# GELU gate by exponential and division, weight split on GpSimd, and row work one step later in a two-block transformer kernel

## The chip, the cores and the metric

The kernel runs on one core of a Trainium2 chip. The metric is the device time of one execution in microseconds (us). The core's engines are TensorE (PE in the profile, with its weight loads as PEld), VectorE (DVE), ScalarE (ACT), GpSimd (POOL) and SyncE (SP), which only issues DMAs here. Each engine works through its own instructions in program order and waits on semaphores for the others.

## What is computed

Two transformer blocks over 1024 rows of 1024 numbers in float32: first an mLSTM and pooling layer and a windowed attention layer, then a block with gated linear attention, differential attention and a feed-forward part with a convolution. The change touches the code of that feed-forward part and the schedule of the output projections. In short:

```python
# the end of each mixer: a product with w_out, added to x, then the norm of the next part
h = h + jnp.concatenate([o_gla, o_diff], axis=-1) @ w_out[i]
h = h + conv_ffn(rms_norm(h, norm_ffn[i]), w_up[i], conv_w[i], conv_b[i], w_down[i])

def conv_ffn(h, w_up, conv_w, conv_b, w_down):       # w_up is 1024 x 5632, w_down 2816 x 1024
    T = h.shape[1]
    u = h @ w_up
    up = jnp.pad(u, ((0, 0), (CONV_W - 1, 0), (0, 0)))
    c = conv_b + sum(up[:, j:j + T] * conv_w[j] for j in range(CONV_W))      # CONV_W = 3
    gate, val = jnp.split(c, 2, axis=-1)
    return (jax.nn.gelu(gate) * val) @ w_down
```

## The kernel before

**Split weights.** Products are made from pairs: each 128x4096 weight slot holds a high part (ScalarE's rounded copy, `split_hi`, L403) and a low part (VectorE's difference, `split_lo`, L412), and TensorE sums three passes of high and low. The same is done for the other operand. There are three weight slots, `K.W[:, 0..2]`, loaded by SyncE; a slot is loaded again when TensorE has finished with its old item.

**Output projections (`rows_part`).** `out0`, `out1`, `out2` and `down` are built by one function. Rows come in tiles of 128; `out1` and `out2` have three groups of tiles, [0,1,2], [3,4,5] and [6,7], with `per` = 4 weight items for each group, so 12 steps s = 0..11. `out0` has `per` = 8 and `down` `per` = 11. After a group's last step its tiles go through this sequence, all 128x1024:

- VectorE adds the old x (L2622 in `out2`; L2629 and L2633 in `out1`), ScalarE makes the norm factor (`act_x`, L559), VectorE scales the tile ("scale", `vec_scale`, L588);
- TensorE turns it by eight 128x128 transposes into the one PSUM tile `TR` ("turn r", `pe_turn`, L633). Turn r waits until the tile before it was read from `TR` (semaphore `ht_done`);
- VectorE multiplies `TR` by the norm gain ("value r", `vec_value`, L610; this raises `ht_done`), ScalarE rounds it ("high r", L618), VectorE makes the difference ("low r", L624).

Which tile is handled at which step is said by `due(s, lag, behind)`. Turns come at lag 1, at the end of a step: tiles 3, 4, 5 are turned at the ends of steps 9, 10 and 11. Value and high use lag 2, low uses lag 3, each one step more where `behind` applies. Within one step VectorE's order is: low parts that are due; adds; the split of this step's weights; at s = 11 also the split of the first item of the next part (`following[0]` in `out1`; `tail[2](v, 0)`, the first up-projection weights, in `out2`); scale; value. The next part's first item can only be loaded once step 9's weights are free.

**Up projection (`up_part`).** 22 column tiles j. For each, `w_up` brings 128 gate and 128 value columns (two DMAs), double buffered in two of the three weight slots: `load_up` for tile j waits until TensorE finished tile j-2. ScalarE makes the high part (`up_w_hi`, L3515) and VectorE the low one (`up_w_lo`, L3520). TensorE makes unit (j, 0), the gate half, and (j, 1), the value half, each 48 matmuls in four PSUM buffers of two banks. For tiles 0 and 1 it makes the first 512 rows of all four units (interleaved with the last two turns of `out2`), then the second 512 rows. Per half, ScalarE takes the centre tap from PSUM (L3627) and VectorE adds the other two (L3652, L3654). The gate then goes: square on ScalarE (L3632), one product on VectorE (L3667), four functions on ScalarE (L3634 to L3637: Relu, Exp, Ln, Exp, which give a sigmoid), the gate product on VectorE (L3669), and at the end the product with the value half (L3676). `down` starts when the last tile's units are made; its step 1 needs weights and operands that VectorE splits after it has finished tile 21 (L3676).

GpSimd issues the loads and stores of x rows (`B.queue`, L526 and L530) and waits at the end of each `rows_part` until all stores have landed; it does no arithmetic in the parts from `out1` on but for two masks.

Of the kernel before, what the change touches and what calls it, by code (L numbers as in the profile page):

```python
# [29 lines left out]
ALU = mybir.AluOpType  # L30
ACT = mybir.ActivationFunctionType
# [2399 lines left out]
def rows_part(K, st, name, key, groups, turned, source, n_store, gg_rows=None, stream=None, ready=None, raw=None, raw_at=0,  # L2431
# [13 lines left out]
    def due(s, lag, behind=0):  # L2445

        for g, rs in enumerate(groups):
            stride = 2 if per >= 8 and g + 1 < len(groups) else 1
            inside = per * (g + 1) + 4 + stride * (len(rs) - 1) < len(steps)
            wait = lag + behind if inside else lag  # L2450
            n, late = divmod(s - per * (g + 1) - wait, stride)
            if late == 0 and 0 <= n < len(rs):
                yield rs[n]
# [160 lines left out]
    def vector(v):  # L2614
# [20 lines left out]
        for s in range(len(steps) + 6):  # L2635
# [6 lines left out]
            if s == len(steps) and following:  # L2642
                K.split_lo(v, following[1])
            if s == len(steps) + 3 and tail is not None:
                tail[2](v, 1)
            for r in ended(s)[:1] if per >= 8 else ended(s):
# [886 lines left out]
def up_part(K, st, rows):  # L3533
# [19 lines left out]
    s_c, s_sq, s_arg, s_e, s_at = (K.sem("up_centre"), K.sem("up_square"), K.sem("up_gelu_arg"),  # L3553
                                   K.sem("up_gelu_sigmoid"), K.sem("up_act_ready"))

# [11 lines left out]
    def sync(sp):  # L3567
        for j in range(2, NJ):
            K.wait_unit(sp, ("up", j - 2, 1))
            load_up(K, sp, j, K.up_in[j % 2])  # L3570
        for j in (NJ - 2, NJ - 1):
            K.wait_unit(sp, ("up", j, 1))
            K.load_item(sp)
        sp.wait_ge(s_cg, 1)

    def tensor(pe):
# [35 lines left out]
    def scalar(a):  # L3612
        ch = Chain(a, K.a_chain, K.an)
        rows.done(a)
        for j in range(NJ):
            if 2 <= j and j + 1 < NJ:
                up_w_hi(K, a, j + 1)
# [3 lines left out]
            for half, c in ((0, cg), (1, cv)):  # L3621
# [7 lines left out]
                if half == 0:  # L3629
                    K.wait_read(a, key)  # L3630
                    at = K.AT[:, j, :]
                    a.activation(at, cg[:, j % 2, :], ACT.Square, scale=math.sqrt(CUBE)).then_inc(s_sq, 1)  # L3632
                    a.wait_ge(s_arg, j + 1)
                    ch.link(a.activation(at, at, ACT.Relu, scale=SLOPE, bias=K.cut[:, :]))  # L3634
                    ch.link(a.activation(at, at, ACT.Exp, scale=-1.0, bias=K.cut[:, :]))
                    ch.link(a.activation(at, at, ACT.Ln, bias=K.one[:, :]))
                    a.activation(at, at, ACT.Exp, scale=-1.0).then_inc(s_e, 1)  # L3637
                    if j == 0:
                        up_w_hi(K, a, 2)
        K.an = ch.n  # L3640

    def vector(v):
        ch = Chain(v, K.v_chain, K.vn)
        rows.done(v)

        def conv(j, half, c):
# [11 lines left out]
        for j in range(NJ):  # L3658
            at, g = K.AT[:, j, :], cg[:, j % 2, :]
            if 2 <= j and j + 1 < NJ:  # L3660
                up_w_lo(K, v, j + 1)
            if j == NJ - 1:
# [3 lines left out]
            v.wait_ge(s_sq, j + 1)  # L3666
            v.scalar_tensor_tensor(out=at, in0=at, scalar=1.0, in1=g, op0=ALU.add, op1=ALU.mult).then_inc(s_arg, 1)  # L3667
            v.wait_ge(s_e, j + 1)
            ch.link(v.tensor_tensor(at, at, g, ALU.mult))  # L3669
            if j == 0:  # L3670
                up_w_lo(K, v, 2)
            if j == NJ - 1:
# [17 lines left out]

    return Part(sync, None, tensor, scalar, vector, None, (), None, done, taken, left)

# [186 lines left out]
def phase_gla_in(K):  # L3879
# [17 lines left out]
    with ExitStack() as st:  # L3897
# [13 lines left out]
        @block.gpsimd  # L3911
        def _(g):
            out1.gpsimd(g)
            diff.gpsimd(g)
            out2.gpsimd(g)
            down.gpsimd(g)
            ple.gpsimd(g)
# [65 lines left out]
```

## Time and profile before

| | |
|---|---|
| median of 3 runs | 3419.11 us (3415.29 to 3421.77) |
| profiled execution | 3419.11 us, its span 3417.3 us |
| PE busy | 3295.9 us (96%) |
| DVE busy | 1765.1 us (52%) |
| ACT busy | 1508.5 us (44%) |
| POOL busy | 100.3 us (3%) |
| mean granted TensorE clock | 0.988 |

The span runs from the first to the last instruction; 1.8 us of the profiled execution lie around it. Busy times are sums over the whole program and say little of a single part: `out1` lies at about 1863 to 1966 us, `out2` ends at 2520, the up projection ends at 3015, and `down` follows.

### The profile page before, as it was taken

The numbers are of one execution on the slowest core, as the hardware profiler recorded it, in microseconds if no ns is written. First come the engines' busy times: TensorE is split into PE (matmuls) and PEld (weight loads), VectorE is DVE, ScalarE is ACT, GpSimd is POOL, SyncE is SP. The second block draws the span as 40 slices with busy tenths as digits, with TensorE's granted clock in tenths as the row PEclk, the third lists the DMA queues.
The fourth block names the chain that finished last, engine by engine and source line by source line (L and its number), as shares of the span: only waits on it lengthen the run. The fifth ranks groups of instructions, "written<-read, shape, count | busy, mean of one in ns | idle before, by whom it ended". The sixth has DMA issues, their size and how long they took to land. (4 is left out here: it accounts for less than half of the span.)

```text
span 3417.3 us, 42752 instructions
## 1 busy us (share of the span) xinstructions
PE 3295.9 (96%) x17536; PEld 2667.1 (78%) x17536; DVE 1765.1 (52%) x2730; ACT 1508.5 (44%) x2409; POOL 100.3 (3%) x224
## 2 busy tenths in 40 slices
PE   6999999999999999999999999998999999999997
PEld 4988888888777777888787777776778888878775
DVE  6644444445344367541886644348555444544544
ACT  4343433435323345215786534227435444443454
POOL 0000000000000000001000000000000000000000
PEclk9999999999999999999999999999999999999998
DMA  5102011121333456222301711010332111134453
GB/s 202 58 13 81 28 53 56 41 68 38 141 105 134 174 207 249 67 50 68 94 2 34 195 56 50 26 54 1 124 112 61 49 43 44 50 130 160 177 186 129
DMA packets 188533, 308.38 MB, mean 90 GB/s; under 512 B 28369, under 2 KB 122643, under 8 KB 188211
## 3 DMA queue, kind: packets, MB, share of 16 engines
q1 hardware_dynamic: 166275, 226.27, 20.6%
q0 software_dynamic: 19424, 74.14, 6.0%
q10 hardware_dynamic: 2640, 5.24, 0.4%
q8 instruction: 139, 2.28, 0.3%
q14 instruction: 55, 0.45, 0.0%
HBM read 269.87 MB, written 35.75 MB: 89 GB/s over the span
## 5 line engine op out<-in xcount | busy, mean ns | idle before, releaser
L412 DVE TENSOR_TENSOR W_rounded<-W,W_rounded 128x2048 fp32r<-128x2048 f32 (+1 forms) x172 | 348.8, 2029 | 443.4 <-ACT W_rounded L403 440.3
L403 ACT ACTIVATE W_rounded<-W 128x2048 fp32r<-128x2048 f32 (+1 forms) x172 | 292.4, 1701 | 398.6 <-DMA W<-in_w_down 96.9
L3583 PE MATMUL G<-HT_rounded,W_rounded 128*128 128x512 f32 x1584 | 452.7, 393 | 0.0
L3583 PEld LDWEIGHTS G<-HT_rounded,W_rounded 128*128 128x128 f32 x1584 | 298.3, 188 | 68.4
L2547 PE MATMUL G<-W_rounded,r_y_rounded 128*128 128x512 f32 x960 | 229.4, 399 | 6.4 <-DVE r_y_rounded L2653 5.1
L2547 PE MATMUL G<-W_rounded,x_hi 128*128 128x512 f32 x704 | 221.1, 395 | 3.6 <-DVE act_turned_rounded L2653 3.4
L2547 PEld LDWEIGHTS G<-W_rounded,r_y_rounded 128*128 128x128 f32 x960 | 181.1, 190 | 51.7 <-DVE W_rounded L412 6.2
L1147 PE MATMUL G<-W_rounded,HT_rounded 128*128 128x512 f32 x640 | 213.7, 415 | 0.0
L2200 PE MATMUL G<-HT_rounded,W_rounded 128*128 128x512 f32 (+1 forms) x768 | 209.2, 357 | 2.9 <-DVE W_rounded L412 2.9
L3583 PE MATMUL G<-HT_lo_ffn,W_rounded 128*128 128x512 f32 x528 | 208.5, 395 | 0.0
L1191 PE MATMUL G<-HT_rounded,W_rounded 128*128 128x512 f32 (+1 forms) x768 | 205.7, 354 | 1.0 <-PEq L651 1.0
L2870 PE MATMUL G<-W_rounded,HT_rounded 128*128 128x512 f32 x640 | 203.1, 399 | 0.0
L2547 PEld LDWEIGHTS G<-W_rounded,x_hi 128*128 128x128 f32 x704 | 132.4, 189 | 35.3 <-DVE W_rounded L412 4.4
L2200 PEld LDWEIGHTS G<-HT_rounded,W_rounded 128*128 128x128 f32 x768 | 137.5, 189 | 28.2 <-DVE W_rounded L412 3.9
L1191 PEld LDWEIGHTS G<-HT_rounded,W_rounded 128*128 128x128 f32 x768 | 136.0, 188 | 22.6 <-issue 1.2
L2870 PEld LDWEIGHTS G<-W_rounded,HT_rounded 128*128 128x128 f32 x640 | 118.4, 188 | 28.2 <-issue 2.0
L2547 PE MATMUL G<-W_rounded,act_turned_rounded 128*128 128x512 f32 x352 | 139.9, 397 | 0.0
L1147 PEld LDWEIGHTS G<-W_rounded,HT_rounded 128*128 128x128 f32 x640 | 120.2, 188 | 25.2
L2200 PE MATMUL G<-HT_lo,W_rounded 128*128 128x512 f32 (+1 forms) x384 | 137.1, 357 | 0.0
L1191 PE MATMUL G<-HT_lo,W_rounded 128*128 128x512 f32 (+1 forms) x384 | 136.4, 355 | 0.0
L1646 PE MATMUL G<-W_rounded,HT_rounded 128*128 128x512 f32 x416 | 131.6, 397 | 0.2 <-DVE W_rounded L412 0.2
L2870 PE MATMUL G<-W_rounded,o_turned_lo 128*128 128x512 f32 x320 | 126.1, 394 | 0.0
(461 smaller groups left out, 6456.3 us busy)
## 6 DMA issues: line engine op xcount, KB each, us to landing
W<-in_w_down SPq DMA_DIRECT2D x33, 1024.0 KB, 4.8
W<-in_ab_w_out SPq DMA_DIRECT2D x32, 1024.0 KB, 5.5
W<-in_w_up SPq DMA_DIRECT2D x44, 512.0 KB, 5.1
W<-in_ab_w_in SPq DMA_DIRECT2D x20, 1024.0 KB, 8.1
W<-in_w_mod SPq DMA_DIRECT2D x8, 2048.0 KB, 8.2
x_rows<-r_xt POOLq DMA_DIRECT2D x32, 512.0 KB, 5.4
W<-in_c_w_out SPq DMA_DIRECT2D x24, 512.0 KB, 7.2
r_xt<-x_rows POOLq DMA_DIRECT2D x24, 512.0 KB, 4.8
```

Of the source, the lines that this page charges most:

```text
L403: ins = a.activation(self.half(key, True)[:, at], self.half(key, False, False)[:, at], ACT.Copy)
L412: ins = v.tensor_tensor(self.half(key, False)[:, at], self.half(key, False, False)[:, at], self.half(key, True)[:, at].bitcast(F32), ALU.s ...
L1147: ins = pe.matmul(G[:, K.par(key), :], x[y][:, 4 * kh + k, r * P:(r + 1) * P], wv[z][:, k, :], start=(kh == 0 and k == 0 and (y, z) == SPL ...
L1191: ins = pe.matmul(G[:, K.par(key), 0:n], wv[y][:, k, cc], x[z][:, k, c0:c0 + n], start=(k == 0 and (y, z) == SPLIT_PASSES[0]), stop=(k == ...
L1646: ins = pe.matmul(bank(key), x[y][:, 4 * kh + k, r * P:(r + 1) * P], w[z][:, k, :], start=(kh == 0 and k == 0 and (y, z) == SPLIT_PASSES[0 ...
L2200: ins = pe.matmul(bank(key, n), w[y][:, k, cc], x[z][:, k, c0:c0 + n], start=(k == 0 and (y, z) == SPLIT_PASSES[0]), stop=(k == KT - 1 and ...
L2547: ins = pe.matmul(slot(r)[:, n * 512:(n + 1) * 512], x[y], w[z][:, k, n * 512:(n + 1) * 512], start=(kk == 0 and k == 0 and (y, z) == SPLI ...
L2870: ins = pe.matmul(bank(key), x[y][:, 4 * kh + k, r * P:(r + 1) * P], w[z][:, k, :], start=first, stop=last)
L3583: ins = pe.matmul(bank(("up", j, half))[:, rc * 512:rc * 512 + 512], w[a][:, k, c], x[b][:, 2 * rc:2 * rc + 2, :], start=(k == 0 and a == ...
```

## The change

Three things are changed. In `up_part` the sigmoid is made as 1 / (1 + exp(-SLOPE z)): one exponential on ScalarE, then an addition of 1 and a reciprocal on VectorE; the cubic argument is made by VectorE in two instructions. The low parts of the up-projection weights for j = 1 to 21 are made by GpSimd (a new `gpsimd` function that stands behind `out2`'s in GpSimd's queue), and `up_w_hi(2)` moves from the inside of iteration 0 to the head of iteration 1. In `rows_part`, `due` gives the extra step to every group but the last. For `out0` (`per` 8) and `down` (`per` 11) the old and the new rule give the same steps; for `out1` and `out2` the values, highs and lows of tiles 3, 4, 5 move from steps 10, 11, 12 (values, highs) and 11, 12, 13 (lows) to one step later each.

```diff
--- before.py
+++ after.py
@@ -2445,9 +2445,8 @@
     def due(s, lag, behind=0):
 
         for g, rs in enumerate(groups):
+            wait = lag + behind if g + 1 < len(groups) else lag
             stride = 2 if per >= 8 and g + 1 < len(groups) else 1
-            inside = per * (g + 1) + 4 + stride * (len(rs) - 1) < len(steps)
-            wait = lag + behind if inside else lag
             n, late = divmod(s - per * (g + 1) - wait, stride)
             if late == 0 and 0 <= n < len(rs):
                 yield rs[n]
@@ -2641,8 +2640,6 @@
                         B.vec_lo(v, r)
             if s == len(steps) and following:
                 K.split_lo(v, following[1])
-            if s == len(steps) + 3 and tail is not None:
-                tail[2](v, 1)
             for r in ended(s)[:1] if per >= 8 else ended(s):
                 add(r)
             if s < len(steps):
@@ -3551,7 +3548,7 @@
     first = K.pl.units[("up", 0, 0)]
     s_cg = K.sem("up_last_gate")
     s_c, s_sq, s_arg, s_e, s_at = (K.sem("up_centre"), K.sem("up_square"), K.sem("up_gelu_arg"),
-                                   K.sem("up_gelu_sigmoid"), K.sem("up_act_ready"))
+                                   K.sem("up_gelu_exp"), K.sem("up_act_ready"))
 
     def bank(key):
         return G[:, (K.pl.units[key] - first) % 4, :]
@@ -3572,6 +3569,10 @@
             K.wait_unit(sp, ("up", j, 1))
             K.load_item(sp)
         sp.wait_ge(s_cg, 1)
+
+    def gpsimd(g):
+        for j in range(1, NJ):
+            up_w_lo(K, g, j)
 
     def tensor(pe):
         def piece(j, half, rc):
@@ -3610,10 +3611,9 @@
                 piece(j, half, 1).then_inc(K.gemm_done, 1)
 
     def scalar(a):
-        ch = Chain(a, K.a_chain, K.an)
         rows.done(a)
         for j in range(NJ):
-            if 2 <= j and j + 1 < NJ:
+            if 1 <= j and j + 1 < NJ:
                 up_w_hi(K, a, j + 1)
             if j == NJ - 1:
                 K.split_hi(a, ("down", 0, 0))
@@ -3628,21 +3628,13 @@
                              bias=K.col("conv_b_2", tile)).then_inc(s_c, 1)
                 if half == 0:
                     K.wait_read(a, key)
-                    at = K.AT[:, j, :]
-                    a.activation(at, cg[:, j % 2, :], ACT.Square, scale=math.sqrt(CUBE)).then_inc(s_sq, 1)
+                    a.activation(K.AT[:, j, :], cg[:, j % 2, :], ACT.Square).then_inc(s_sq, 1)
                     a.wait_ge(s_arg, j + 1)
-                    ch.link(a.activation(at, at, ACT.Relu, scale=SLOPE, bias=K.cut[:, :]))
-                    ch.link(a.activation(at, at, ACT.Exp, scale=-1.0, bias=K.cut[:, :]))
-                    ch.link(a.activation(at, at, ACT.Ln, bias=K.one[:, :]))
-                    a.activation(at, at, ACT.Exp, scale=-1.0).then_inc(s_e, 1)
-                    if j == 0:
-                        up_w_hi(K, a, 2)
-        K.an = ch.n
+                    a.activation(K.AT[:, j, :], K.AT[:, j, :], ACT.Exp, scale=-SLOPE).then_inc(s_e, 1)
 
     def vector(v):
         ch = Chain(v, K.v_chain, K.vn)
         rows.done(v)
-
         def conv(j, half, c):
 
             key = ("up", j, half)
@@ -3657,18 +3649,17 @@
 
         for j in range(NJ):
             at, g = K.AT[:, j, :], cg[:, j % 2, :]
-            if 2 <= j and j + 1 < NJ:
-                up_w_lo(K, v, j + 1)
             if j == NJ - 1:
                 K.split_lo(v, ("down", 0, 0))
                 K.early[1](v)
             conv(j, 0, cg)
             v.wait_ge(s_sq, j + 1)
-            v.scalar_tensor_tensor(out=at, in0=at, scalar=1.0, in1=g, op0=ALU.add, op1=ALU.mult).then_inc(s_arg, 1)
+            ch.link(v.tensor_scalar(at, at, CUBE, 1.0, ALU.mult, ALU.add))
+            v.tensor_tensor(at, at, g, ALU.mult).then_inc(s_arg, 1)
             v.wait_ge(s_e, j + 1)
+            ch.link(v.tensor_scalar(at, at, 1.0, None, ALU.add))
+            ch.link(v.reciprocal(at, at))
             ch.link(v.tensor_tensor(at, at, g, ALU.mult))
-            if j == 0:
-                up_w_lo(K, v, 2)
             if j == NJ - 1:
                 v.tensor_copy(K.zcol[:, 1:2], K.eps[:, :]).then_inc(s_cg, 1)
             conv(j, 1, cv)
@@ -3688,7 +3679,7 @@
 
         K.wait_unit(eng, ("up", NJ - 1, 1))
 
-    return Part(sync, None, tensor, scalar, vector, None, (), None, done, taken, left)
+    return Part(sync, gpsimd, tensor, scalar, vector, None, (), None, done, taken, left)
 
 
 def phase_up(K):
@@ -3913,6 +3904,7 @@
             out1.gpsimd(g)
             diff.gpsimd(g)
             out2.gpsimd(g)
+            up.gpsimd(g)
             down.gpsimd(g)
             ple.gpsimd(g)
 
```

## Rows read from the trace of the kernel before

**Rows 1.** Windows of all engines: busy us of PE, PEld, DVE, ACT, POOL, clock, DMA.
```profile
2600.00:3000.00 400.00, 400.00 (x1734) 325.21 (x1733) 204.54 (x148) 182.29 (x148) 0.00 (x0) 1.00 0.17 48
```

**Rows 2.** Timeline of PE, `out1`'s end: start us, us, engine, line, operation, [idle before <-releaser].
```profile
1958.12 1.03 PE L633 MATMUL TR<-ident,r_xs 128*128 128x128 f32 x8
...
1978.30 1.09 PE L633 MATMUL TR<-ident,r_xs 128*128 128x128 f32 x8 [1.26 <-DVE r_xs L588]
```

**Rows 3.** Timeline of ACT, the high part of `out1`'s `following[0]`.
```profile
1957.22 1.92 ACT L403 ACTIVATE W_rounded<-W 128x2048 fp32r<-128x2048 f32 x1 [0.31 <-DMA W<-in_w_in]
```

**Rows 4.** Timeline of DVE, `out1`'s step 11.
```profile
1956.95 4.52 DVE L412 TENSOR_TENSOR W_rounded<-W,W_rounded 128x2048 fp32r<-128x2048 f32 x2 [0.58 <-ACT W_rounded L403]
...
1962.05 1.21 DVE L610 TENSOR_TENSOR r_h_turned<-TR,cols 128x1024 f32<-128x1024 f32 x1
```

**Rows 5.** Timeline of DVE, `out2`'s step 11: first up split, scale 5, value 4.
```profile
2515.20 2.29 DVE L3520 TENSOR_TENSOR W_rounded<-W,W_rounded 128x2048 fp32r<-128x2048 f32 x1 [3.92 <-ACT W_rounded L3515]
2517.41 0.75 DVE L588 TENSOR_SCALAR r_xs<-r_xt,r_ss 128x1024 f32<-128x1024 f32 x1
2518.07 1.22 DVE L610 TENSOR_TENSOR row_room<-TR,cols 128x1024 f32<-128x1024 f32 x1
```

**Rows 6.** Timeline of PE, `out2`'s end: the turns of tiles 4 to 7.
```profile
2510.23 1.03 PE L633 MATMUL TR<-ident,r_xs 128*128 128x128 f32 x8
...
2519.44 1.06 PE L633 MATMUL TR<-ident,r_xs 128*128 128x128 f32 x8 [2.23 <-DVE row_room L610]
...
2529.18 1.97 PE L633 MATMUL TR<-ident,r_xs 128*128 128x128 f32 x8 [3.16 <-DVE r_xs L588]
...
2538.26 1.03 PE L633 MATMUL TR<-ident,r_xs 128*128 128x128 f32 x8
```

**Rows 7.** Windows of PE alone behind two of its waits: PE busy, clock, DMA, GB/s.
```profile
1945.00:1952.00 7.00, 7.00 (x27) 0.81 0.86 239
...
2529.00:2535.00 6.00, 5.82 (x18) 0.52 0.27 107
```

**Rows 8.** DMA issues of the page: KB each, median us from issue to landing.
```profile
x_rows<-r_xt POOLq DMA_DIRECT2D x32, 512.0 KB, 5.4
```

**Rows 9.** Groups of POOL by line and shape: busy us, mean ns, idle before.
```profile
L1060 POOL MEMSET k_rows<- 68x1280 f32 x1 | 1.2, 1164 | 70.8 <-POOLq L651 70.8
```

**Rows 10.** Timeline of ACT, high part of the up weights of tile 2.
```profile
2567.13 1.92 ACT L3515 ACTIVATE W_rounded<-W 128x2048 fp32r<-128x2048 f32 x1 [0.19 <-DMA W<-in_w_up]
```

**Rows 11.** Timeline of PE where unit (1, 1) ends and (2, 0) begins.
```profile
2570.72 2.01 PE L3583 MATMUL G<-HT_rounded,W_rounded 128*128 128x512 f32 x8
```

**Rows 12.** Timeline of DVE, the split before tile 21 to `down`'s step 1.
```profile
3000.38 2.29 DVE L412 TENSOR_TENSOR W_rounded<-W,W_rounded 128x2048 fp32r<-128x2048 f32 x1 [1.63 <-ACT W_rounded L403]
...
3005.90 1.28 DVE L3652 SCALAR_TENSOR_TENSOR W<-G,cols,W 128x1023 f32<-128x1023 f32 x1 [2.36 <-ACT W L3627]
...
3009.63 1.23 DVE L3667 SCALAR_TENSOR_TENSOR act_turned<-act_turned,W 128x1024 f32<-128x1024 f32 x1 [1.13 <-ACT act_turned L3632]
3015.53 1.23 DVE L3669 TENSOR_TENSOR act_turned<-act_turned,W 128x1024 f32<-128x1024 f32 x1 [4.67 <-ACT act_turned L3637]
...
3019.62 1.23 DVE L3676 TENSOR_TENSOR act_turned<-act_turned,W 128x1024 f32<-128x1024 f32 x1
3022.55 2.29 DVE L412 TENSOR_TENSOR W_rounded<-W,W_rounded 128x2048 fp32r<-128x2048 f32 x1 [1.71 <-ACT W_rounded L403]
```

**Rows 13.** Groups by line and shape: a reciprocal of two columns, the gate product, ScalarE's last Exp.
```profile
L1994 DVE RECIPROCAL sums<-sums 128x2 f32<-128x2 f32 x64 | 10.2, 160 | 2.2 <-ACT HT L1954 2.2
...
L3669 DVE TENSOR_TENSOR act_turned<-act_turned,W 128x1024 f32<-128x1024 f32 x22 | 26.9, 1225 | 102.9 <-ACT act_turned L3637 102.9
...
L3637 ACT ACTIVATE act_turned<-act_turned 128x1024 f32<-128x1024 f32 x22 | 23.3, 1060 | 0.7
```

**Rows 14.** Instructions of line 922: min/median/max ns, first and last start.
```profile
L922 DVE RECIPROCAL silu_c<-silu_c x1: 253/253/253, 13.9 to 13.9; 128x16 f32<-128x16 f32 x1
```

**Rows 15.** Timeline of PE, `down`'s step 1.
```profile
3025.86 0.82 PE L2547 MATMUL G<-W_rounded,x_hi 128*128 128x512 f32 x2 [1.92 <-DVE act_turned_rounded L2653]
```

## Prediction

> **What bounds the kernel now.** I read the windows of all engines first: how full is each engine where the change works, and at which clock? Over 400 us of the up projection TensorE is busy for all 400 at full clock, with 1734 matmuls, so 0.231 us each and 22.1 us for the 96 of a column tile, while DVE has 205 us of work and ACT 182 [rows 1]. There the path to the end is TensorE's own queue. Taking work off ScalarE or VectorE brings nothing in that stretch; time can only be lost or won where TensorE waits. So I read TensorE's timeline around every place that the change touches (the ends of `out1` and `out2`, the first tiles of the up projection, the step into `down`), and then, for each wait, the timelines of DVE and ACT to see what was late.
>
> **The extra step for tiles 3 to 5, in `out1`.** Turn 4 stands at the end of step 10 and needs value 3, since `TR` is one tile. Before, value 3 was made in VectorE's step 10 and turn 4 ran at 1958.12 without a wait [rows 2]. After, value 3 stands in step 11, behind that step's split, the split of `following[0]`, and scale 5. This slot is held by a load: the high part of `following[0]` starts at 1957.22 when its DMA has landed, ends at 1959.14 [rows 3], the low part takes half of the 4.52 of two splits [rows 4], to 1961.4, then scale 5 at 0.75 [rows 5]. The slot is thus the one where value 4 stood, 1962.05 to 1963.26 [rows 4]. Turn 4 can start at about 1963.4, 5.3 us late, and behind TensorE nothing else can go: step 11 and turn 5 queue behind it. Given back: the wait of 1.26 at turn 6 [rows 2], as ScalarE and VectorE catch up while TensorE stands. The matmuls behind a wait run partly at the lower clock level: behind a wait of 3.16 us [rows 6] the windows show a mean clock of 0.52 over 6 us, 2.9 us lost; behind one of 2.95 us, 0.81 over 7 us, 1.3 us lost [rows 7]. For the longer waits of this change I take 2.9, with 1.3 as the lower end. `out1`: 5.3 - 1.3 + 2.9 = **+6.9**.
>
> **The same in `out2`.** Value 3 moves behind `tail[2](v, 0)`, which waited 3.92 us for ScalarE's high part (and that for its DMA) and began at 2515.20; scale 5 follows, and the slot at 2518.07 is value 4's now [rows 5]. It released turn 5 at 2519.44; after, the same slot releases turn 4 at 2519.44, which used to run at 2510.23 [rows 6]. The wait is 9.2 us and swallows the old one of 2.23. Step 11 and one turn are left to do that before were done: 24 matmuls x 0.231 and eight transposes in about 1 us [rows 6], 6.5 us. By then scale 6 and value 5 are made (two adds, scale, value, some 5 us of VectorE), so the wait of 3.16 at turn 6 [rows 6] goes. Its lower clock goes too (2.9) and comes back behind the longer wait (2.9). `out2`: 6.5 - 3.2 = **+3.3**; lower end 1.7 with 1.3 for the clock.
>
> The removed `tail[2](v, 1)` frees 2.3 us of VectorE behind turn 6, where TensorE then waits for nothing: 0. GpSimd makes that low part instead, behind its wait until the last store has landed, 5.4 us after its issue [rows 8]. The last add is at about 2529, so it can start near 2535 and has until turn 7 is over, 2538.26 [rows 6] + 3.3 + 1.0 = 2542.6: 7 us for one instruction. That costs nothing below that price.
>
> **The low parts on GpSimd.** No row shows a two-input operation on POOL. Its memset writes 1280 columns in 1.164 us [rows 9], so 2048 columns are 1.86 us for one stream; a subtraction moves three streams, 5.6 us if each takes its turn. I take 4.5, near the upper end, since the memset reads nothing. The page GPSIMD Engine Reference of the Trainium skill, section 3.1, gives 4.5 us for a two-input operation of this size on GpSimd against 2.3 on VectorE; the trace shows only the VectorE side. In the steady state this hides: the weights of tile 2 landed 5.9 us after the unit that freed them (2567.13 less 2572.34 - 11.1) [rows 10, 11]; from tile 3 on TensorE needs them 22.1 us after that unit, and 22.1 - 5.9 - 1.9 = 14.3 are left for GpSimd; without that cover each tile would pay the excess. The tight place is tile 2, whose weights can be loaded only when unit (0, 1) is done, 11 us before they are needed. The high part starts at 2567.13 when the DMA has landed, and ends at 2569.05 [rows 10]. Of the eight matmuls from 2570.72 the last is the first of unit (2, 0), so it is at 2572.34 [rows 11]. With two handovers of 0.1 us, 3.1 us are left. Stall: 4.5 - 3.1, about **+1.5** (ends 0 and 2.6). `up_w_hi(2)` at the head of iteration 1 stands behind the centre tap of unit (0, 1), which is over before the DMA lands: 0.
>
> **The gate.** Between the start of L3667 and that of L3669 lie 5.90 us before [rows 12]. After, the same stretch holds an addition and scaling 0.75 and a product 1.23, one Exp 1.06, an addition 0.75 [rows 5, 12, 13], and a reciprocal of 1024 columns. Sixteen columns took 0.253 us, two 0.160 [rows 13, 14]: 6.6 ns a column, 6.9 us. The ends are far: 1.2 if it ran like a product, 16 if the whole 0.253 were columns. I take the slope. Sum 10.7, with handovers 10.9: +5.0 for each tile. VectorE then works about 19.7 us a tile (15.0 before, from 3005.90 to 3020.85 [rows 12], plus 5.0 less a wait of 0.3), below 22.1, so the up projection stays TensorE's, with 2.4 us to spare.
>
> **The step into `down`.** Tile 20 ends 5.0 late; the gaps of 1.63 and 2.36 around the split [rows 12] take 4.0 and a 0.3 of wait inside the tile, so tile 21 starts 0.7 late and ends 5.7 late. Then `down`'s step-1 split no longer waits 1.71 for ScalarE [rows 12]. TensorE's wait of 1.92 [rows 15] grows by 5.7 - 1.7 = **+4.0**. For the clock I add half of 2.9 - 1.3: **+0.8**. Lower end 0 (a cheap reciprocal), upper 6.5.
>
> **Sum.** 6.9 + 3.3 + 1.5 + 4.0 + 0.8 = 16.5 us. The profiled execution took 3419.11 with a span of 3417.3, 1.8 around it, and is itself the median: **3435.6 us**, 0.48% slower. About 0.2% (6.8 us) is what a measurement of this kernel can tell from no change.
>
> **Rivals.**
> - *The turns do not wait.* If value 3 were made before TensorE asks, only 1.5 + 4.8 remain: 3425.4. It decides at 1958.1 and 2510.2, so loads would have to land 5 and 9 us earlier. The releasers speak against it. This is the one that ends on the other side, not slower by 0.2%. Chance 0.07.
> - *The longer waits cost no clock.* With nothing lost behind either turn wait: 16.5 - 2.9 - 2.9 - 0.8 = +9.9, 3429.0. Chance 0.1.
> - *GpSimd and VectorE hold each other up.* Each low part on GpSimd meets a two-input product of VectorE. A product held for up to 4.5 us, less the 2.4 spare in a tile, ends tile 21 some 2 us later, and a held start at tile 2 adds up to 1.2: 3438.8. Nothing before has both engines at work, so the trace is silent. This is what SBUF — State Buffer in the Trainium skill, section "Who interferes with whom", would have: a VectorE instruction with two SBUF inputs and a GpSimd one that reads SBUF exclude each other. Chance 0.2.
> - *GpSimd is far slower than its bound,* 9 us or more (held at each step): tile 2 waits 6, with 2.9 of clock, and VectorE is pushed by up to 4.5 at the end: +12 on the sum, 3448. It would set the pace only above 14.3. Chance 0.08.
> - *VectorE becomes the bound.* Above a reciprocal of 9.3 us its tile exceeds 22.1; at 10.3 some 20 tiles lose 1 us each: 3456. The slope speaks against it. Chance 0.05.
> - *My sum:* 0.5.
>
> **Range.** 3424 to 3447 takes in the first three rivals with the lower ends (5.3 + 1.7 + 0 + 0 = 7.0, 3426) and the upper ones. Slower by over 0.2%: my sum, the second to the fifth rival, less their low edges: 0.85. Within: 0.12, from the first rival and the low ends together. Faster: 0.03, since no wait before leaves 7 us to win at these places.
>
> **What would show it.** In the new profile: turn 4 of `out1` (L633) waits about 5 us, and of `out2` about 9, for the value in L610; turn 6 in both waits for nothing; clock windows below 1 behind both; a POOL TENSOR_TENSOR of some 4.5 us at L3520, 21 times; TensorE waits about 1.5 us for it at tile 2 and never after; a RECIPROCAL of about 6.9 us, 22 times; TensorE waits about 6 us at `down`'s step 1. I am wrong if value 3 is reached earlier, if the reciprocal's slope does not hold at 1024 columns, or if DVE instructions stretch beside POOL's.

## The result

The changed kernel took 3439.14 us (median of 4 runs, 3433.74 to 3442.89), the kernel before 3420.34 us beside it (4 runs). The ratio is 1.0054, with a 95% interval of 1.0041 to 1.0066: slower by 18.8 us by the medians and by 14 to 22.6 by the interval. The prediction had 3435.6 us in a range of 3424 to 3447. The profiled execution took 3436.55 us, its span 3434.8.

### The profile page after: what moved, and what is told of

Its sections match the earlier page's. It is cut to its first block and busy times, and to the rows that moved or that the text cites. A ratio compares the mean times of both kernels' runs of the same rounds, so it can differ in the third digit from the quotient of the medians.

```text
span 3434.8 us, 42754 instructions
## 1 busy us (share of the span) xinstructions
PE 3296.7 (96%) x17536; PEld 2668.0 (78%) x17536; DVE 1944.5 (57%) x2775; ACT 1430.8 (42%) x2343; POOL 198.2 (6%) x245
## 5 line engine op out<-in xcount | busy, mean ns | idle before, releaser
L1191 PEld LDWEIGHTS G<-HT_rounded,W_rounded 128*128 128x128 f32 x768 | 136.0, 188 | 22.6 <-issue 1.2
L3661 DVE RECIPROCAL act_turned<-act_turned 128x1024 f32<-128x1024 f32 x22 | 144.2, 6553 | 0.8
```

The lines of the kernel that those rows point to most:

```text
L1191: ins = pe.matmul(G[:, K.par(key), 0:n], wv[y][:, k, cc], x[z][:, k, c0:c0 + n], start=(k == 0 and (y, z) == SPLIT_PASSES[0]), stop=(k == ...
L3661: ch.link(v.reciprocal(at, at))
```

## The profile after

Where the 17.5 us between the two spans arose is read from TensorE's timeline, at places that both kernels have: the first matmul of `out1` and of `down`, and the turns of tiles 3 and 7. The places of before that [rows 2, 6] do not show are from the same timeline. Each stretch is the difference of two starts.

| stretch on TensorE | before | after | difference |
|---|---|---|---|
| start to `out1` | 1863.84 | 1865.38 | +1.5 |
| `out1` to its turn 7 | 120.97 | 123.83 | +2.9 |
| to `out2`'s turn 3 | 518.95 | 517.12 | -1.8 |
| to `out2`'s turn 7 | 34.50 | 37.24 | +2.7 |
| to `down`'s start | 477.27 | 478.75 | +1.5 |
| `down` to the end of the span | 401.8 | 412.5 | +10.7 |

The first and the third row hold hardly any instruction that the change touches: 1.5 and -1.8 us there are the scatter of one execution against another. The second row mixes the change with such scatter. Up to the turn of tile 3, ahead of any moved instruction, `out1` took 87.9 us before and 85.1 after; from there to the turn of tile 7 it took 33.1 and 38.8. So the change itself costs 5.7 us in `out1`. The prediction had 6.9, 3.3, 1.5 and 4.8 for the four others.

The page of the changed kernel, busy time and share by engine (its first and third line):

```profile
span 3434.8 us, 42754 instructions
...
PE 3296.7 (96%) x17536; PEld 2668.0 (78%) x17536; DVE 1944.5 (57%) x2775; ACT 1430.8 (42%) x2343; POOL 198.2 (6%) x245
```

TensorE's work is the same as before (3295.9). DVE has 179 us more, ACT 78 less, POOL 98 more. TensorE is idle for 138.1 us of the span, 121.4 before. These 16.7 us are nearly all of the 17.5; its busy time, which holds what a lower clock costs anywhere in the program, grew by 0.8.

The timeline of PE, both turns of tile 4; columns as in [rows 2]:

```profile
1961.82 1.94 PE L633 MATMUL TR<-ident,r_xs 128*128 128x128 f32 x8 [4.20 <-DVE r_h_turned L610]
```

```profile
2521.91 1.94 PE L633 MATMUL TR<-ident,r_xs 128*128 128x128 f32 x8 [8.94 <-DVE row_room L610]
```

Where [rows 2, 6] have turn 4 without a wait, it waits now for value 3, in both parts. Turn 6, which waited 1.26 and 3.16 us, waits for nothing. These two turns take 1.94 us each, where [rows 2] has 1.03: the clock is low, as it was for the turn behind 3.16 us in [rows 6]. The windows of PE alone behind them, and behind the first matmul of `down`'s step 1 (columns as in [rows 7]):

```profile
1961.00:1969.00 8.00, 7.18 (x25) 0.61 0.13 51
...
2521.00:2529.00 8.00, 7.09 (x25) 0.62 0.00 0
...
3039.00:3047.00 8.00, 7.03 (x19) 0.57 0.10 41
3047.00:3053.00 6.00, 6.00 (x28) 1.00 0.10 14
```

Behind each of the three waits the engine is busy 7 of 8 us at a mean clock near 0.6, so at 1.2 GHz for most of the stretch, and is back at 2.4 GHz in the next 6 us. That is some 3 us each, as [rows 7] had behind a wait of 3.16.

Why value 3 comes late stands in DVE's timeline at the end of `out1` and of `out2`:

```profile
1957.58 2.29 DVE L412 TENSOR_TENSOR W_rounded<-W,W_rounded 128x2048 fp32r<-128x2048 f32 x1 [2.43 <-ACT W_rounded L403]
1959.79 0.75 DVE L588 TENSOR_SCALAR r_xs<-r_xt,r_ss 128x1024 f32<-128x1024 f32 x1
1960.45 1.22 DVE L610 TENSOR_TENSOR r_h_turned<-TR,cols 128x1024 f32<-128x1024 f32 x1
...
2517.68 2.29 DVE L3517 TENSOR_TENSOR W_rounded<-W,W_rounded 128x2048 fp32r<-128x2048 f32 x1 [5.29 <-ACT W_rounded L3512]
2519.88 0.75 DVE L588 TENSOR_SCALAR r_xs<-r_xt,r_ss 128x1024 f32<-128x1024 f32 x1
2520.55 1.22 DVE L610 TENSOR_TENSOR row_room<-TR,cols 128x1024 f32<-128x1024 f32 x1
```

The slot is the predicted one: behind a split that waits for the next part's weights, and behind scale 5. In `out1` that load landed 1.6 us earlier (ScalarE's high part starts at 1955.63, not 1957.22 as in [rows 3]), and TensorE was ready for the turn 0.5 us earlier, so the wait is 4.20 and not 5.3.

Now the step into `down`. TensorE's list of waits from 2560 to 3060 us is short (engine, tile, line, releaser: total us, times, longest):

```profile
PE G L2546 <- DVE act_turned_rounded L2650: 9.2, 1, 9.2
PE G L3584 <- POOL W_rounded L3517: 1.2, 1, 1.2
```

The second is tile 2, predicted at 1.5. The first was 1.92 [rows 15] and predicted at about 6; here is the step that went wrong. The groups of the up projection by line and shape (busy us, mean ns, idle before), first two of VectorE, then one of GpSimd:

```profile
L3661 DVE RECIPROCAL act_turned<-act_turned 128x1024 f32<-128x1024 f32 x22 | 144.2, 6553 | 0.8
L3662 DVE TENSOR_TENSOR act_turned<-act_turned,W 128x1024 f32<-128x1024 f32 x22 | 76.3, 3469 | 0.8
...
L3517 POOL TENSOR_TENSOR W_rounded<-W,W_rounded 128x2048 fp32r<-128x2048 f32 x21 | 97.5, 4644 | 359.8 <-ACT W_rounded L3512 357.3 <-DMA x_rows<-r_xt 2.4
```

Two prices that the old trace did not show came out near their estimates: the reciprocal 6.55 us (6.9), GpSimd's subtraction 4.64 (4.5). But the gate product, 1.225 us in [rows 13], has a mean of 3.47. One tile of it in the timelines of DVE and POOL:

```profile
2980.63 6.55 DVE L3661 RECIPROCAL act_turned<-act_turned 128x1024 f32<-128x1024 f32 x1
2987.22 4.15 DVE L3662 TENSOR_TENSOR act_turned<-act_turned,W 128x1024 f32<-128x1024 f32 x1
2991.40 1.28 DVE L3644 SCALAR_TENSOR_TENSOR W<-G,cols,W 128x1023 f32<-128x1023 f32 x1
```

```profile
2985.66 4.62 POOL L3517 TENSOR_TENSOR W_rounded<-W,W_rounded 128x2048 fp32r<-128x2048 f32 x1 [17.46 <-ACT W_rounded L3512]
```

GpSimd starts during the reciprocal and ends at 2990.28. The product starts at 2987.22 and ends at 2991.37, 1.1 us after GpSimd's end, which is about its own usual length: it makes no headway until GpSimd's instruction is over. The same is seen in the 20 tiles whose product overlaps a low part of GpSimd: each product ends 1.07 to 1.10 us after GpSimd's instruction, however long it has been under way (1.33 to 4.69 us). The page SBUF — State Buffer of the Trainium skill, section "Who interferes with whom", says that a VectorE instruction with two SBUF inputs and a GpSimd one that reads SBUF exclude each other; the trace agrees, with these numbers.

What the holds leave behind, in DVE's timeline of tiles 20 (first line) and 21:

```profile
3009.30 1.23 DVE L3662 TENSOR_TENSOR act_turned<-act_turned,W 128x1024 f32<-128x1024 f32 x1
...
3017.41 1.28 DVE L3644 SCALAR_TENSOR_TENSOR W<-G,cols,W 128x1023 f32<-128x1023 f32 x1
...
3035.53 1.23 DVE L3667 TENSOR_TENSOR act_turned<-act_turned,W 128x1024 f32<-128x1024 f32 x1
3036.67 2.28 DVE L412 TENSOR_TENSOR W_rounded<-W,W_rounded 128x2048 fp32r<-128x2048 f32 x1
```

`down` starts at 3022.32 on TensorE. Against that, tile 21's first tap starts at -4.9 (before -9.6, from 3005.90 and 3015.53 in [rows 12] and the table) and its last product at +13.2 (before +4.1). So VectorE comes to tile 21 4.7 us late, the gate adds 4.4, together 9.1. The two gaps of 1.63 and 2.36 us in [rows 12] are gone, and so is the one of 1.71 before the last split. 9.1 less 1.8 for that last one is 7.3, and 1.92 + 7.3 is the wait of 9.2.

The 4.7 us are not the last hold alone. The table has how much later than in the kernel before VectorE starts a tile's first tap, each kernel measured from its own first matmul of `down` (us; `pool_later`, an experiment below, keeps GpSimd's low parts off the product from tile 10 on):

| tile | 3 | 4 | 5 | 10 | 11 | 12 | 20 | 21 |
|---|---|---|---|---|---|---|---|---|
| changed kernel | 6.8 | 5.7 | 4.8 | 4.7 | 4.7 | 4.7 | 4.7 | 4.7 |
| `pool_later` | 6.8 | 5.8 | 4.9 | 4.8 | 1.8 | 0.0 | 0.0 | 0.1 |

VectorE comes late out of the first tiles. Where nothing holds it, it makes up 3 us a tile. In the changed kernel the hold takes just these 3 us from each tile: a product that starts 1.0 us after GpSimd takes 4.69 us, one that starts 2.0 us after it 3.68. So VectorE stays behind to the end.

## The experiments

Each kernel is compared with the kernel before on the same chip. Line numbers are those of each kernel and differ by a few.

### Each part alone

`rows_only` is the kernel before with the new `due`; `gate_and_pool` is the changed kernel with the old one. `gate_only` puts only the new gate into the kernel before. `pool_only` is `gate_and_pool` with the old gate.

```diff
 # in short
 rows_only                     (gate_and_pool: the reverse, in the changed kernel)
-            inside = per * (g + 1) + 4 + stride * (len(rs) - 1) < len(steps)
-            wait = lag + behind if inside else lag
+            wait = lag + behind if g + 1 < len(groups) else lag
 gate_only
-        Square, scalar_tensor_tensor, Relu, Exp, Ln, Exp
+        Square, tensor_scalar, tensor_tensor, Exp, tensor_scalar, reciprocal
 pool_only                     (against the kernel before)
+    def gpsimd(g):
+        for j in range(1, NJ):
+            up_w_lo(K, g, j)
```

> The kernel before with nothing but the new rule in due (values, highs and lows of tiles 3 to 5 one step later in out1 and out2). My theory: this is a part of its own, worth what the markers of the changed kernel show for it: TensorE's offset to before grows by about 3 us over out1 (turn 4 waits about 4, turn 6 no longer waits) and by about 2.7 us over out2 (turn 4 waits 9, the waits of 2.2 and 3.2 go), so +6 us, 3426. Rival A (the later values cost nothing by themselves and only matter beside GpSimd's part): within 1 us of before. Rival B (the clock behind the waits makes it dearer): +9 to +10 as I had summed.

> The changed kernel with the old rule in due. My theory: the rest of the loss, +1.2 at tile 2 and +7 to +10 at down's step 1 with its clock, so +10 to +12 us, 3431; the wait at down's step 1 stays at about 9 us. Rival (the parts lean on each other): the wait at down is near 6 and the sum of this run and rows_only is more than 3 us away from the whole change's 17 to 19.

> The kernel before with the gate by exponential and reciprocal, but low parts of the up weights on VectorE as before, old order, old due. VectorE's tile is then 19.5 us plus the low part's 2.3, 21.8, just under TensorE's 22.1. My theory: no instruction of VectorE is stretched (products at 1.22 us), but its low parts come late at tiles 2 and 3 (waits of about 3 us each, with some lower clock) and the wait at down's step 1 is 5 to 7 us: +10 to +13 us. Rival (the reciprocal alone is harmless as long as GpSimd does not touch SBUF): +4 or less, from down's step 1 alone.

> The changed kernel with the old gate (four functions on ScalarE, no reciprocal) and the old due: only the low parts are on GpSimd. My theory: VectorE has 9 us to spare per tile, so a held product costs nothing; TensorE waits about 1.2 us at tile 2, the wait at down's step 1 is near its old 1.9: +1 to +2 us, within noise of before. Rival (GpSimd's part alone makes the loss by holding VectorE): the wait at down's step 1 grows to 5 or more and the time by +5 or more.

| kernel | median us (runs) | before us | ratio | interval |
|---|---|---|---|---|
| `rows_only` | 3429.87 (5) | 3416.83 | 1.0034 | 1.0021 to 1.0047 |
| `gate_and_pool` | 3429.17 (8) | 3416.83 | 1.0037 | 1.0024 to 1.0049 |
| `gate_only` | 3428.55 (11) | 3416.83 | 1.0033 | 1.0021 to 1.0045 |
| `pool_only` | 3421.14 (12) | 3416.83 | 1.0009 | 0.9998 to 1.0020 |

TensorE's waits of `rows_only` at the end of `out1`, at the end of `out2`, and at `down`:

```profile
PE TR L633 <- DVE r_h_turned L610: 5.2, 1, 5.2
...
PE TR L633 <- DVE row_room L610: 9.1, 1, 9.1
...
PE G L2546 <- DVE act_turned_rounded L2652: 2.1, 1, 2.1
```

Those of `gate_and_pool` at `out2` and from 2560 us on, and last that of `gate_only` at `down`:

```profile
PE TR L633 <- DVE r_xs L588: 3.1, 1, 3.1
PE TR L633 <- DVE row_room L610: 1.8, 1, 1.8
...
PE G L2547 <- DVE act_turned_rounded L2651: 9.4, 1, 9.4
PE G L3585 <- POOL W_rounded L3518: 1.4, 1, 1.4
...
PE G L2547 <- DVE act_turned_rounded L2653: 4.5, 1, 4.5
```

The waits part cleanly. The new `due` alone makes the two waits of turn 4 and leaves `down` at 2.1; the gate with GpSimd leaves `out2` as it was and makes 9.4 at `down`. `gate_only` has 4.5 at `down`, its gate product takes 1.225 us on the mean, and its waits at tiles 2 and 3 come to 3.8 us, for VectorE's low parts this time. `pool_only` has 1.9 at `down` and 2.0 at tile 2, and no time that its interval tells from no change; it also holds the moved `up_w_hi(2)` and the removed `tail[2](v, 1)`. Its held instruction is the final product of a tile (mean 1.71 us), and VectorE has the slack for it. So neither half of the second part makes the 9.4 by itself: the gate alone gives 4.5, GpSimd alone nothing, both together 9.4.

Against the expectations: `gate_and_pool` (10 to 12 expected) and `gate_only` (10 to 13) came about as expected, +12.3 and +11.7 us, though the wait of `gate_only` at `down` is 4.5 and not 5 to 7. `rows_only` did not: 6 us were expected, read off two rows of the first table, and it lost 13.0, at least 7 by its interval. `pool_only` has 4.3 by the medians where 1 to 2 were expected, with an interval of -0.7 to 6.8.

In `rows_only`, `out1` to its turn 7 took 126.57 us and `out2` from turn 3 to turn 7 37.44: +5.6 and +2.9 against before, where the changed kernel had +2.9 and +2.7. From turn 3 to turn 7 of `out1` the two kernels agree, +6.2 and +5.7. The difference lies ahead of turn 3 and can be read: in the 75 us from 1860 on, ahead of any moved instruction, the profiled execution of before and that of `rows_only` had a mean granted clock of 0.95, that of the changed kernel 0.98, which is 2.2 us of head start for the latter.

The two halves come to 13.0 and 12.3 us by their medians and the whole to 18.8, whose interval ends at 22.6. The intervals of the halves, 7 to 16 and 8 to 17 us, allow that. Of the rival that the parts lean on each other, one sign came (the sum is more than 3 us off) and the other did not (the wait at `down` stays 9.4). Whether a few us are shared between the halves is not settled by these runs.

### Is it the hold?

`pool_later` is `gate_and_pool` with GpSimd's low part held back, from tile 12 on, until VectorE has made the final product of tile j - 2; what it meets then are taps, whose one tensor input is in PSUM and the other in SBUF, and not the gate product. `no_reciprocal` is `gate_and_pool` with the reciprocal replaced by a minimum with 1.0; it leaves out the division of the gate.

```diff
 pool_later
         for j in range(1, NJ):
+            if j >= 12:
+                g.wait_ge(s_at, j - 1)
             up_w_lo(K, g, j)
 no_reciprocal
-            ch.link(v.reciprocal(at, at))
+            ch.link(v.tensor_scalar(at, at, 1.0, None, ALU.min))
```

> As gate_and_pool, but from tile 12 on GpSimd starts a low part only when VectorE has finished the tile two before, so that its instruction no longer falls on the gate product behind the reciprocal. My theory (VectorE's product is held until GpSimd's instruction has ended): the product at that place drops from 4.2 us to 1.22 from there on, VectorE's last tile ends about 3 us earlier, the wait at down's step 1 falls from 9.4 to about 6 as I had predicted, and with it the time by 3 to 4 us against gate_and_pool; GpSimd still finishes before TensorE asks. Rival (VectorE's lateness at the end comes from the reciprocal alone, the long product only fills a gap): the product gets short but the wait at down stays above 8.5.

> As gate_and_pool, with the reciprocal replaced by a minimum with 1.0 of the same shape, which leaves the division out (the gate factor is then 1). My theory: VectorE's tile falls to about 14 us, GpSimd's low part meets no two-input product any more, the wait at down's step 1 goes back to about 2, and what is left against before is the 1.4 of tile 2: +1 to +2 us. Rival (GpSimd's low part holds VectorE wherever it falls): stretched VectorE instructions remain and the wait at down stays at 4 or more.

`pool_later` took 3423.82 us (12 runs) against 3416.71, ratio 1.0020 (1.0009 to 1.0030). `no_reciprocal` took 3417.07 (10 runs), 0.9998 (0.9987 to 1.0008). Of `pool_later`, the timeline of DVE at the tile shown above, then that of POOL, then the wait at `down`:

```profile
2976.17 6.55 DVE L3664 RECIPROCAL act_turned<-act_turned 128x1024 f32<-128x1024 f32 x1
2982.76 1.23 DVE L3665 TENSOR_TENSOR act_turned<-act_turned,W 128x1024 f32<-128x1024 f32 x1
...
2990.80 1.28 DVE L3647 SCALAR_TENSOR_TENSOR W<-G,cols,W 128x1023 f32<-128x1023 f32 x1 [2.91 <-ACT W L3630]
```

```profile
2987.96 4.62 POOL L3518 TENSOR_TENSOR W_rounded<-W,W_rounded 128x2048 fp32r<-128x2048 f32 x1 [17.52 <-DVE act_turned L3670]
```

```profile
PE G L2547 <- DVE act_turned_rounded L2651: 4.5, 1, 4.5
```

Nothing changed but the time at which GpSimd starts, from tile 12's low part on. The product is back at 1.23 us, VectorE has 2.91 us of slack in a tile again, and the wait at `down` falls from 9.4 to 4.5, which is what `gate_only` had. By the medians that is 12.3 to 7.1 us of loss; the two intervals overlap, so the time alone would not settle it, but the product and the wait do; in the two profiles `down` to the end of the span takes 409.0 and 405.0 us. The instruction on GpSimd takes 4.62 us whether it meets the product or not: where GpSimd has started first, only VectorE gives way. The expectation had about 6 left at `down`; 4.5 were.

`no_reciprocal` keeps GpSimd early. Its low parts take 4.61 us, a few final products are held (mean 1506 ns), and `down` waits 2.1 us. The expectation had no held product left; but with the 6.55 us out of VectorE's tile, a hold finds slack to fall into and costs nothing that is measured. So the loss at `down` needs the reciprocal, which alone takes the wait from 1.9 to 4.5; the hold takes it from there to 9.4.

### The order of VectorE's queue in step 11

If turn 4 of `out2` waits only because value 3 stands behind the split for the next part, then that split moved behind scale and value should give the time back, with the new `due` still in place. `rows_tail_last` does so to `rows_only`, `tail_last` to the kernel before.

```diff
-                if tail is not None:
-                    tail[2](v, 0)
 ...                                   # scale and value of this step
+            if s == len(steps) - 1 and tail is not None:
+                tail[2](v, 0)         # and the same for ScalarE's tail[1](a, 0)
```

> As rows_only (new rule in due), but in out2's step 11 both halves of the first up split stand behind scale, value and high of that step, on ScalarE and on VectorE. My theory (value 3 is late only because it stands behind a split that waits for a load): the wait at out2's turn 4 falls from 9.1 to about 2, out1 keeps its 5.2, and out2's part of the loss goes: +7 or so in all instead of +11. Rival (the extra step itself, not what stands in it, is the price): turn 4 still waits 8 or more.

> The kernel before with the same order of step 11 in out2 (the first up split behind scale, value and high), old due. If the waits at out2's end come from work standing behind the load of the first up weights, turn 5 no longer waits 2.2, turn 6 waits less than 3.2, the lower clock behind them may go, and the kernel is 2 to 6 us faster than before, near what can be measured. Rival (the first up weights are then late themselves): TensorE waits for L3520 at unit (0, 0) instead and the time is the same.

`rows_tail_last` took 3421.77 us (10 runs) against 3416.71, ratio 1.0009 (0.9997 to 1.0020), where `rows_only` had 1.0034. Its waits at the end of `out2`, and its values 3 and 4 in DVE's timeline:

```profile
PE TR L633 <- DVE row_room L610: 3.6, 3, 1.7
PE G L3582 <- DVE W_rounded L3519: 1.7, 1, 1.7
```

```profile
2510.88 1.22 DVE L610 TENSOR_TENSOR row_room<-TR,cols 128x1024 f32<-128x1024 f32 x1
2515.19 2.29 DVE L3519 TENSOR_TENSOR W_rounded<-W,W_rounded 128x2048 fp32r<-128x2048 f32 x1 [3.09 <-ACT W_rounded L3514]
...
2518.79 1.23 DVE L610 TENSOR_TENSOR row_room<-TR,cols 128x1024 f32<-128x1024 f32 x1
```

Value 3 now stands ahead of the split that waits for its weights, and the one wait of 9.1 us becomes 1.67, 1.25 and 0.63 us at turns 4, 5 and 6, and 1.7 for the split itself at the first unit that needs it. `out1`, where the order is untouched, still waits 5.2, and `down` 2.0. Out of some 13 us, 8 are back (5.1 left), and the intervals of the two ratios just part. That is more than the 2.9 us which the new `due` had added in `out2`, since the order also does away with waits that the kernel before has there, 2.23 and 3.16 us with the clock behind the second [rows 6, 7]. From `out2`'s turn 3 to `down`'s start `rows_only` takes 514.7 us, `rows_tail_last` 509.1, the kernel before 511.8: 5.6 of the 8 us are seen there. `tail_last` took 3415.52 us (12 runs), 0.9995 (0.9984 to 1.0005). Turn 5 no longer waits, turn 6 still does, 2.9 us. 2 to 6 us were expected; in its one profile that stretch is 3.2 us shorter than before, but in time nothing can be measured.

### Both repairs in the changed kernel

```diff
 the changed kernel, with the edits of pool_later and of rows_tail_last
```

> The whole changed kernel with the two repairs that were tried one by one: GpSimd's low parts held back behind the tile's gate from tile 12 on, and in both row parts' last step the split for the next part moved behind scale 5 and value 3. If the losses that the single runs showed are separate, the changed kernel's +18.6 us shrinks by about 8 (the order in the rows: 3429.9 to 3421.8) and about 5 (the hold: 3429.2 to 3423.8), to some +5 to +8: about 3425. Waits then: turn 4 of out1 still about 5, turn 4 of out2 about 1.7, tile 2 about 1.3, step 1 of down about 4.5. Rival: the two parts hide each other, since the row part's delay is partly taken up before down; then one repair brings nothing on top of the other and the time stays at 3431 or above.

It took 3425.95 us (8 runs) against 3413.84 beside it, ratio 1.0032 (1.0019 to 1.0046). TensorE's waits over the row parts and the up projection, in the same view as above:

```profile
PE TR L633 <- DVE row_room L610: 6.0, 4, 2.0
...
PE TR L633 <- DVE r_h_turned L610: 5.4, 1, 5.4
PE G L2546 <- DVE act_turned_rounded L2650: 4.5, 1, 4.5
...
PE G L3586 <- POOL W_rounded L3517: 1.4, 1, 1.4
```

The expectation speaks of both row parts; the edit moves the split in `out2` alone. The waits are the expected ones but for one: turn 7 of `out2` now waits 2.0 us as well. The median is the expected 3425, but the kernel before was also 3 us faster on this chip, so the loss is 12.1 us and not 5 to 8; the interval (6.5 to 15.7) reaches into that. The two repairs recover something of the 18.8 us, 0.0022 of the ratio or 7.5 us by its middle (the two intervals still meet, the waits are clear); that they recover all 13 which they brought one by one is not shown. No version that was run beats the kernel before.

Where each kernel's time is, read from the one profile of each at the places of the first table (us; the last column is the difference of the medians):

| kernel | `out1`, turn 3 to 7 | `out2`'s turn 3 to `down` | `down` to the end | median against before |
|---|---|---|---|---|
| before | 33.1 | 511.8 | 401.8 | |
| changed | 38.8 | 516.0 | 412.5 | +18.8 |
| `rows_only` | 39.3 | 514.7 | 403.4 | +13.0 |
| `gate_and_pool` | 33.1 | 511.7 | 409.0 | +12.3 |
| `gate_only` | 33.3 | 517.6 | 409.4 | +11.7 |
| `pool_only` | 33.8 | 515.7 | 402.5 | +4.3 |
| `pool_later` | 33.3 | 513.3 | 405.0 | +7.1 |
| `no_reciprocal` | 33.2 | 513.0 | 400.3 | +0.4 |
| `rows_tail_last` | 39.0 | 509.1 | 402.5 | +5.1 |
| `tail_last` | 33.1 | 508.6 | 402.8 | -1.2 |
| `both_repairs` | 39.2 | 511.5 | 406.8 | +12.1 |

The first column falls into two groups, 33.1 to 33.8 with the old `due` and 38.8 to 39.3 with the new one, whatever else is changed. So `both_repairs` keeps the 6 us of `out1`, which neither repair touches, and about 5 in `down`, behind the wait of 4.5. The last column but one scatters by 3 us among the kernels whose wait at `down` is near 2 (400.3 to 403.4), and `gate_only` and `pool_later`, with the same wait of 4.5, are 4.4 apart: a single profile is good for some 3 to 4 us there.

## Why the prediction held, and where it did not

**TensorE sets the pace; time is lost only where it waits.** Right. From 2620 to 3020 us TensorE is busy for all 400 us at full clock after the change too, though DVE went from 205 us [rows 1] to 355.

**`out1`, +6.9.** The place, the slot and the releaser are as predicted. The wait was 4.2 us in the changed kernel and 5.2 in `rows_only` (5.3 predicted), the wait at turn 6 is gone (-1.3), the clock lost some 3 us (2.9). From turn 3 to turn 7 that is +5.7 and +6.2 us. The term was about 1 us too large.

**`out2`, +3.3.** Measured +2.7 and +2.9, with a wait of 8.9 and 9.1 (9.2 predicted), none at turn 6, and the same clock behind it. Right.

**Tile 2 on GpSimd, +1.5.** 1.2 us here, 1.4 in `gate_and_pool`. GpSimd's 4.64 us against my 4.5 and the 3.1 available give it. Right, and TensorE never waited for GpSimd again.

**The gate, +5.0 a tile, and `down`, +4.0 and +0.8.** This is the term that was mis-sized: `down` lost 10.7 us, not 4.8. The part of it that my sum described is what `gate_only` and `pool_later` show, a wait of 4.5 (5.9 predicted, from a gate that is 4.4 us longer and not 5.0, and a tile 21 that begins 0.1 us late and not 0.7). On top came the hold of VectorE's product by GpSimd, named as a rival with a chance of 0.2 and priced at 2 us at tile 21; it brought VectorE to tile 21 4.7 us late and the wait to 9.2. The rival set the 4.5 us against 2.4 of slack in a tile and kept the remainder, 2 us, once. Measured, the product lost 2.9 us in each tile, which is all the slack that VectorE has there (2.91 in `pool_later`). It never made up the lateness of the first tiles and carried it into tile 21, where the 4 us of gaps around the split were already spent on the gate. Of the other 3.4 us in `down` the clock behind the longer wait explains about 1.8: 0.57 over 8 us, where before it was 0.79. The remaining 1.6 is as large as the scatter of the unchanged stretches. In `gate_and_pool`, with a wait of 9.4, `down` grew by 7.2 us only, so the term was too small by 2.4 to 5.9.

**The sum.** 16.5 predicted, 20.6 at the four places (5.7 + 2.7 + 1.5 + 10.7). The spans differ by 17.5 only because the profile before was 3.1 us slower where the change does nothing (2.8 ahead of `out1`'s turn 3, 1.8 and -1.5 elsewhere). So the terms of the row parts were right in mechanism and, within 1.2 us, in size, `down` was too small by up to 5.9, and part of the nearness of 3435.6 to 3439.14 is luck.

**The rivals.** The turns do wait (first rival). The waits do cost clock (second). GpSimd at 4.64 and the reciprocal at 6.55 us rule out the fourth and the fifth. The third holds, and its time of 3438.8 is the nearest to the measured 3439.14; its mechanism is shown by `pool_later`. Its size was wrong: it had VectorE 2 us later at tile 21 for the hold, and 4.6 were measured (4.7 against 0.1), while the 1.2 us that it added for a held start at tile 2 did not come (the whole wait there is 1.2). That its time fits so well is chance.

## What to carry to other kernels

An engine with idle time is not free to take work: ask at which hand-over the added microseconds arrive, and add them there, since VectorE, busy for 355 of 400 us, cost nothing in the stretch and made a wait of 9 us at its end. When GpSimd is given a pass over SBUF beside VectorE, look up which VectorE instructions it will overlap, and start it where none with two SBUF inputs is due; one wait in GpSimd's queue did that here, and gave back 5 us of TensorE's wait. In an engine's in-order queue, work that the critical engine waits for should not stand behind an instruction that waits for a load.

## What the runs showed of the hardware

- A reciprocal of 128x1024 float32 takes 6.55 us on VectorE, against 1.23 for a product of the same size. With the 0.253 us for 16 columns [rows 14] that is 6.3 ns a column.
- A VectorE product with both inputs in SBUF that starts while GpSimd subtracts (128x2048, 4.6 us, both inputs in SBUF) ends 1.07 to 1.10 us after GpSimd's instruction ends. Most gate products of the changed kernel took over 4 us (median 4.16, longest 4.69, alone 1.22). GpSimd's time is 4.6 us with or without it. The strongest case is a difference of 256 columns in `out2`, in DVE's timeline, beside POOL's first low part:

```profile
2535.10 0.96 DVE L624 TENSOR_TENSOR HT_lo_ffn<-row_room,HT_rounded 128x768 fp32r<-128x768 f32 x1 [1.13 <-ACT HT_rounded L618]
2535.98 4.83 DVE L624 TENSOR_TENSOR HT_rounded<-row_room,HT_rounded 128x256 fp32r<-128x256 f32 x1
...
2544.61 0.42 DVE L624 TENSOR_TENSOR HT_rounded<-row_room,HT_rounded 128x256 fp32r<-128x256 f32 x1
```

```profile
2535.44 5.09 POOL L3517 TENSOR_TENSOR W_rounded<-W,W_rounded 128x2048 fp32r<-128x2048 f32 x1 [2.43 <-DMA x_rows<-r_xt]
```

It stretched from 0.42 to 4.83 us and ended 0.3 us after GpSimd's instruction (2540.53). The difference of 768 columns ahead of it had started before GpSimd and kept its 0.96 us; there it is GpSimd's instruction that took 5.09 us and not 4.6, so in this one case GpSimd gave way to a VectorE instruction that had started first. VectorE's taps, with one input in PSUM, keep their 1.28 us beside GpSimd in `pool_later`. VectorE's reciprocal, with one input, was not stretched by an overlap (6.55 us in `gate_only`, without GpSimd, and in the changed kernel).
